# Keys and values of block 2 as seven half-size products, and one megabyte of an expert's weights in the router's places

## The reference, cut to what matters

```python
u = rmsnorm(h, norm1_g)
proj = u @ w_in                      # 1024 -> 6656 columns
cb, cc, cx, q, k, v, gc, ga = split_columns(proj)   # q 1024 wide, k and v 256 each
...
h = h + merged @ w_o
hf = rmsnorm(h, norm2_g)
# 64 experts of width 512, two per token, chosen from hf @ w_group and hf @ w_router
y = (silu(xb @ w1[e]) * (xb @ w3[e])) @ w2[e]
```

## Time and profile before

| | |
|---|---|
| median of 3 runs | 1544.93 us (1544.66 to 1547.16) |
| the profiled execution | 1545.07 us, of which the span is 1543.2 us |
| PE busy | 1247.8 us (81%) |
| DVE, ACT, POOL busy | 549.4, 246.7, 18.2 us |
| loaded from memory | 499.78 MB, 325 GB/s over the span |
| mean granted TensorE clock | 0.917 of full speed |

### The profile page before, as it was taken

One profiled execution on the slowest core, in us unless ns is written; L12 is line 12 of the kernel. 1 busy time (PEld: TensorE's weight loads), 2 busy tenths in 40 slices (PEclk: granted clock), 3 DMA queues, 4 the chain that ended last, 5 costly groups with the idle time before them and its releaser, 6 DMA issues.

```text
span 1543.2 us, 18891 instructions
## 1 busy us (share of the span) xinstructions
PE 1247.8 (81%) x8005; PEld 706.6 (46%) x8005; DVE 549.4 (36%) x1115; ACT 246.7 (16%) x710; POOL 18.2 (1%) x30
## 2 busy tenths in 40 slices
PE   8999999999999999996765775775676576577477
PEld 5665899944699544542232232232232233223223
DVE  6644578795756667421111111111111111111111
ACT  2434213211234101211010010010000001001001
POOL 2000000000000000100000000000000000000000
PEclk9999999999999999998888898788798789788889
DMA  9631746406433686999999999999999999999997
GB/s 305 217 111 55 244 153 217 162 30 217 163 112 113 236 303 237 374 429 428 429 429 429 428 429 428 428 429 428 429 429 428 428 429 428 429 429 429 429 426 327
DMA packets 93859, 501.53 MB, mean 325 GB/s; under 512 B 6845, under 2 KB 34865, under 8 KB 68464
## 3 DMA queue, kind: packets, MB, share of 16 engines
q1 hardware_dynamic: 93040, 500.00, 79.9%
q0 software_dynamic: 768, 0.85, 0.2%
HBM read 499.78 MB, written 1.05 MB: 325 GB/s over the span
## 4 chain that ended last, share of the span: by engine, by line
PE 58%; DMA 39%; DVE 2%; issue 1%; ACT 1%; SPq 0%; DVEq 0%
DMA arena<-in_w 38%; PE ps L1754 18%; PE ps L1329 8%; PE ps L1558 6%; PE ps L1553 4%; PE ps L1366 3%; PE ps L928 2%; PE ps L1139 2%; PE ps L933 2%; PE ps L978 2%; PE ps L1494 2%; PE ps L1654 1%; PE ps L1279 1%; PE ps L1432 1%; PE ps L955 0%
## 5 line engine op out<-in xcount | busy, mean ns | idle before, releaser
L1754 PE MATMUL ps<-arena,hT 128*32 128x512 f32 x1984 | 277.8, 723 | 252.7 <-DMA arena<-in_w 252.7
L1754 PEld LDWEIGHTS ps<-arena,hT 128*32 128x32 f32 x1984 | 69.2, 130 | 460.8 <-issue 319.3
L3006 DVE TENSOR_TENSOR moe_hid<-moe_hid,ps 64x512 f32<-64x512 f32 x32 | 22.1, 690 | 480.8 <-ACT moe_hid L3407 480.8
L1776 PE MATMUL ps<-arena,moe_turned 128*32 128x512 f32 x1024 | 118.3, 601 | 28.0 <-DVE moe_turned L3008 27.9
L1734 PEld LDWEIGHTS ps<-sel,h 128*128 128x128 f32 x992 | 113.2, 192 | 24.1 <-issue 24.1
L3407 ACT ACTIVATE moe_hid<-ps 64x512 f32<-64x512 f32 x32 | 18.8, 588 | 655.9 <-PE ps L1754 650.3
L1734 PE MATMUL ps<-sel,h 128*128 128x64 f32 x992 | 117.2, 276 | 0.0
L3391 ACT ACTIVATE hT<-ps,gcol 128x64 f32<-128x64 f32 x252 | 55.0, 328 | 156.8 <-PE ps L1734 156.8
L3008 DVE COPY moe_turned<-ps 128x512 f32<-128x512 f32 x32 | 22.1, 692 | 161.8 <-PE ps L1765 161.8
L1776 PEld LDWEIGHTS ps<-arena,moe_turned 128*32 128x32 f32 x1024 | 32.9, 110 | 88.7 <-issue 72.0
L1329 PE MATMUL ps<-arena 128*128 128x128 f32 x640 | 73.1, 275 | 0.0
(11 more groups left out here) (499 smaller groups left out, 1427.3 us busy)
## 6 DMA issues: line engine op xcount, KB each, us to landing
arena<-in_w SPq DMA_DIRECT2D x182, 2048.0 KB, 29.4
arena<-in_w_in SPq DMA_DIRECT2D x18, 2048.0 KB, 9.1
arena<-in_w_up SPq DMA_DIRECT2D x22, 1024.0 KB, 9.0
arena<-in_w SPq DMA_DIRECT2D x17, 1024.0 KB, 12.9
arena<-in_w_down SPq DMA_DIRECT2D x5, 2048.0 KB, 13.5
arena<-in_w_out SPq DMA_DIRECT2D x2, 2048.0 KB, 15.2
arena<-in_w_conv_out SPq DMA_DIRECT2D x2, 2048.0 KB, 7.7
arena<-in_w_attn_out SPq DMA_DIRECT2D x2, 2048.0 KB, 11.9
```

The source lines that it names most:

```text
L1754: last = mm(ps[k * CAP:(k + 1) * CAP, UP, :], x[:, c, (k % 2) * CAP:(k % 2 + 1) * CAP], w[:, at:at + DE], start=(c == 0), stop=(c == KC - 1))
L1776: last = mm(ps[k * CAP:(k + 1) * CAP, DN, :], a[:, m * 64 + (k % 2) * CAP:m * 64 + (k % 2 + 1) * CAP], w[:, at:at + 512], start=(m == 0), ...
```

## The change

1. **Keys and values.** `kv2` becomes seven products of half the rows, half the inner dimension and half the columns (256), in banks 0 to 3, interleaved with those of the queries: kv 1, the first half of q 1, the turn of the tokens, the rest of q 1, kv 2, kv 5, 6, 7, q 2, kv 3, kv 4, q 5, 6, 7, 3, 4. DVE makes the four weight sums of `kv2` around its share of the first token half (`norm_take(2, 0)`), and five sums of results; ACT copies two. `q_first_w_sums` moves behind the left-side sums.
2. **Release.** `release_last` is gone from this place. `dense_used` is raised for `kv2` in product 5 of the queries, after a wait for all seven kv products.
3. **The megabyte.** `xg` shrinks to the first quarter of `hT`. The first half of w3 of expert 3 goes, behind `load_behind_wo` and after the router's products, into the other three quarters of `hT` (0.75 MB) and into `router_w` (0.25 MB). Its second half goes into slot 0 at the first `quarter_used`; the load at the second is gone. In pair 1 `expert_up` takes the fourth matmul's weights from these places.
4. **Pairs 1 and 2** are written out for PE, and the loop has 14 turns for pairs 3 to 30.

The products, sums and outputs are the same otherwise. The core of the diff (the constants for semaphore counts, the tile views and the removed `part` branches are left out):

```diff
+ORDER_Q, ORDER_KV = [1, 2, 5, 6, 7, 3, 4], [1, 2, 5, 6, 7, 3, 4]
...
-        LOOPED = range(1, PAIRS - 1)
+        LOOPED = range(3, PAIRS - 1)
...
-        xg = hT[:, :, 0:2 * CAP]
+        hT_flat = hT.rearrange("p c s -> p (c s)")
+        xg = hT_flat[:, 0:KC * 2 * CAP].rearrange("p (c s) -> p c s", c=KC)
+        ahead = [hT_flat[:, at:at + DE] for at in (512, 1024, 1536)] + [router_w.rearrange("p c n -> p (c n)")[:, 0:DE]]
...
+            def load_ahead():
+                sp.wait_ge(logits_ready, 2)
+                sp.dma_start(hT_flat[:, 512:2048], t["w3"][3, :, 0:3 * DE]).then_inc(piece_in, 16)
+                sp.dma_start(ahead[3], t["w3"][3, :, 3 * DE:4 * DE]).then_inc(piece_in, 16)
...
                         load_behind_wo()
+                        load_ahead()
                         sp.wait_ge(quarter_used, 1)
-                        sp.dma_start(MOE_SLOTS[0][:, 0:2048], t["w3"][3, :, 0:2048]).then_inc(moe_loaded[0], 16)
-                        moe_wait(1, 3)
-                        sp.dma_start(MOE_SLOTS[0][:, 2048:4096], t["w3"][3, :, 2048:4096]).then_inc(moe_loaded[0], 16)
+                        sp.dma_start(MOE_SLOTS[0][:, 0:2048], t["w3"][3, :, 2048:4096]).then_inc(moe_loaded[0], 16)
...
+            def kv(product):
...
+                if product in (5, 6, 7, 4):
+                    pe.wait_ge(kv_summed, count1(KV_SUMS, {5: "t1", 6: "t2", 7: "t3", 4: "t4"}[product]))
...
+                if product == 2:
+                    pe.wait_ge(seven_copied, KV_COPIED)
+                if product in (3, 4):
+                    pe.wait_ge(kv_summed, count1(KV_SUMS, {3: "c22", 4: "u2"}[product]))
+                for c in range(4):
...
+                    last = mm(kv_bank(product), lhs, rhs, start=(c == 0 and product not in (2, 3)), stop=(c == 3),
+                              skip_group_check=True)
+                last.then_inc(kv_filled, 1)
+
+            def queries(product, chunks=range(4)):
...
+                if product in (3, 4):
+                    pe.wait_ge(seven_sums, count7(-1, SUMS7, {3: "c22", 4: "u2"}[product]))
+                for c in chunks:
...
+                    if product == 5 and c == 0:
+                        pe.wait_ge(kv_filled, len(ORDER_KV))
+                        pe.sem_inc(dense_used, 1)
+                if 3 in chunks:
                     last.then_inc(seven_filled, 1)
+
+            def kv_and_queries():
+                wait_hT(16)
+                kv(1)
+                queries(1, (0, 1))
+                norm_turn(2, xn2, 1)
+                queries(1, (2, 3))
+                kv(2)
+                wait_hT(20)
+                for product in (5, 6, 7):
+                    kv(product)
+                queries(2)
+                kv(3)
+                kv(4)
+                for product in (5, 6, 7, 3, 4):
+                    queries(product)
...
+                        if second and k == 3:
+                            w, at = (units[3], (c - 4) * DE) if half else (ahead[c], 0)
...
+            kv_w_sum("t1")
             norm_take(2, 0)
+            for name in ("t3", "t2", "t4"):
+                kv_w_sum(name)
             dve.wait_ge(ff_down, 5)
...
                 v.tensor_tensor(q_x[:, 1], q_x[:, 0], a11, ALU.subtract).then_inc(x_sums7_ready, 1)
+                dve.wait_ge(x_sums7_ready, count7(-1, X_SUMS7, "s2"))
+                v.tensor_tensor(q_x[:, 3], a12, q_x[:, 1], ALU.subtract).then_inc(x_sums7_ready, 1)
+                q_first_w_sums()
+                for name in ("u2", "u3", "c22"):
+                    kv_sum(name)
                 dve.wait_ge(w_sums7_ready, count7(-1, W_SUMS_UP, "t3"))
                 v.tensor_tensor(b12, b22, q_t1, ALU.subtract).then_inc(w_sums7_ready, 1)
...
                 v.tensor_tensor(w_sum_b, b21, b12, ALU.subtract).then_inc(w_sums7_ready, 1)
+                kv_sum("c12")
+                kv_sum("c21")
                 turn_tables()
                 keys()
                 first_w_sums(0, (1,))
...
                 elif kind == "seven":
+                    act.wait_ge(kv_filled, count1(ORDER_KV, 1))
+                    a_(kv_u2, kv_bank(1), ACT.Copy).then_inc(seven_copied, 1)
```

More of the change, by code:

```diff
@@ L168 @@
 ORDER7 = [5, 1, 6, 7, 2, 3, 4]
-SCHEDULE2 += [("part", "kv2", _q) for _q in range(4)] + [("seven", 0, 0)]
+SCHEDULE2 += [("seven", 0, 0)]
 SCHEDULE2 += [("product", "cc", _p) for _p in ORDER7]
@@ L202 @@
 ORDER_UP = [1, 5, 6, 7, 2, 3, 4]
+ORDER_Q, ORDER_KV = [1, 2, 5, 6, 7, 3, 4], [1, 2, 5, 6, 7, 3, 4]
+KV_COPIED = 2 * UP_SETS + 2
+KV_SUMS = ["t1", "t3", "t2", "t4", "u2", "u3", "c22", "c12", "c21"]
 W_SUMS_UP = ["t1", "t3", "t2", "t4"]
@@ L478, in up_seven_bank, with kv_bank, kv_columns @@
             return ps[:, up_bank(m) + BANK7[product], :]
+        def kv_bank(product):
+            return ps[:, BANK7[product], 0:256]
+        def kv_columns():
+            w = dense_slot("kv2").rearrange("p (c n) -> p c n", c=KC)
+            return w[:, 0:4, 0:256], w[:, 0:4, 256:512], w[:, 4:8, 0:256], w[:, 4:8, 256:512]
         def bank7(g, product):
@@ L1473, in attend @@
                         pe.sem_inc(attn2_done, 1)
-            def q_seven():
-                for n in ("q0", "q1"):
-                    pe.wait_ge(dense_loaded[RING_SLOT[UNIT[n]]], dense_loads(UNIT[n]))
-                b11, b12, b21, b22 = q_columns()
[L1481 to L1497, removed]
-                    last.then_inc(seven_filled, 1)
@@ L1578, in _ @@
             for kind, a, q in SCHEDULE2:
[L1579 to L1585, removed]
+                if kind == "product":
                     seven_product(SET[a], q, hT, release_q if a == "cc" else lambda: release_seven(SET[a] - 1))
@@ L1747, in gather_first, with expert_up @@
                     last.then_inc(gathered, 1)
-            def expert_up(x, units, halved, half, done):
+            def expert_up(x, units, halved, half, done, second=False):
                 for c in range(4 * half, 4 * half + 4):
@@ L1838, in pair_step @@
                         wait_unit(p, k)
+                    if p == 1 and not half:
+                        pe.wait_ge(piece_in, 64)
                     if p and not half:
@@ L1897, in pair_turn @@
                 expert_down(aT, units, False, 1, y_filled)
-            pair_step(0)
+            for p in range(LOOPED[0]):
+                pair_step(p)
             with nc.tensor.Fori(0, len(LOOPED) // 2) as i:
-                pair_turn(1, i)
-                pair_turn(2, i)
+                pair_turn(LOOPED[0], i)
+                pair_turn(LOOPED[1], i)
             pair_step(PAIRS - 1)
@@ L2475, in _, with kv_w_sum @@
             norm_rows(2, xn2, 0)
+            def kv_w_sum(name):
+                b11, b12, b21, b22 = kv_columns()
+                if name == "t1":
+                    u = UNIT["kv2"]
+                    dve.wait_ge(dense_loaded[RING_SLOT[u]], dense_loads(u))
+                if name == "t2":
+                    dve.wait_ge(kv_summed, count1(KV_SUMS, "t1"))
+                if name == "t4":
+                    dve.wait_ge(kv_summed, count1(KV_SUMS, "t2"))
+                x, y = {"t1": (b12, b11), "t3": (b22, b12), "t2": (b22, kv_t["t1"]), "t4": (b21, kv_t["t2"])}[name]
+                v.tensor_tensor(kv_t[name], x, y, ALU.subtract).then_inc(kv_summed, 1)
+            kv_w_sum("t1")
             norm_take(2, 0)
+            for name in ("t3", "t2", "t4"):
+                kv_w_sum(name)
             dve.wait_ge(ff_down, 5)
@@ L2523, in queries, with kv_sum @@
                 v.memset(tail[:, 3:4], 0.0).then_inc(roped2, 1)
[L2525 to L2530, removed]
+            def kv_sum(name):
+                dst, r, product = {"u2": (kv_u2, kv_u2, 6), "u3": (kv_u3, kv_u2, 7), "c22": (v2[:, 1, :], kv_u3, 5),
+                                   "c12": (v2[:, 0, :], kv_u2, 3), "c21": (z2[:, 1, 1024:1280], kv_u3, 4)}[name]
+                dve.wait_ge(kv_filled, count1(ORDER_KV, product))
+                if name == "u2":
+                    dve.wait_ge(seven_copied, KV_COPIED)
+                else:
+                    dve.wait_ge(kv_summed, count1(KV_SUMS, {"u3": "u2", "c22": "u3", "c12": "u2", "c21": "u3"}[name]))
+                done = bank_emptied_dve if name == "c21" else kv_summed
+                v.tensor_tensor(dst, r, kv_bank(product), ALU.add).then_inc(done, 1)
             def cw2(tap, c):
@@ L2799, in q_sum @@
                 v.tensor_tensor(dst, r, ps[:, 4 + BANK7[product], :], ALU.add).then_inc(seven_sums, 1)
-            dve.wait_ge(hT_act, 20)
-            q_first_w_sums()
             for kind, a, q in SCHEDULE2:
-                if kind == "part":
-                    if q % 2 and PRODUCTS[PROD[a]][1][q // 2] == "D":
-                        empty2(a, q // 2)
-                elif kind == "product":
+                if kind == "product":
                     if a == "cc":
@@ L3247, in _ @@
             norm_take(2, 1)
-            def empty2(name, bank):
-                b = filled_bank(name, bank)
```

(8 more changed lines are left out.)

66 lines of the change are left out of this document (48 added, 18 removed).

## The result

The changed kernel takes 1553.22 us (median of six runs, 1551.45 to 1554.68) against 1545.71 us for the kernel before on the same chip (1544.66 to 1547.71): 1.0046 times as long, 95% interval 1.0036 to 1.0056. The forecast was 1551.0 us and "slower"; the first median lies 0.2 us above its range, the second inside it.

A forecast was written before the change was run, and what follows sets the result against it. PE bounds the kernel to about 670 us, then loads set the end, so PE's dense-part time counts. 1545.07 - 1.65 + 5.99 + 2.2 - 0.6 = 1551.0 us; 0.80 chance within 1547.5 to 1553.0.

The forecast's parts named there:

- 6 to 7 were named as a sign: Sign in the changed profile: the first `cc` product comes 6 to 7 us later than 411.07.
- Fewer columns: kv2 on PE: 56 instructions of 256 columns take 12.08 us in place of 13.73, saving 1.65 us.
- The sums of kv: kv's weight sums and copies on DVE and ACT lie beside PE and cost nothing; up to 0.7 us without cover.
- The later release: `cc1` issued at 392.37 reaches DVE at 401.66; the queries' c22 comes late, and PE waits 5.99 us before product 3.
- The clock: PE's granted clock falls in the wait, slowing the queries' products 3 and 4: 2.2 us, range 1.5 to 3.0.
- The rival in which it holds: The clock holds through PE's gap: 1547.7 to 1549.4 us, chance 0.18.
- the one in which it stays low through both products: Clock stays at 1.2 GHz through the queries' products 3 and 4: 6.87 us more, 1556.3 us, chance 0.03.
- The megabyte: Loads ahead fill part of a 0.72 MB hole from 641 to 649 us: 0.6 us gained, range 0 to 1.7.
- That `cc1` would not hold DVE: Rival: `cc1` is in place when DVE asks at 397.7, PE waits only 2.0 us: 1544.8 us, chance 0.11.
- The point from which PE's lost microseconds pass to the end: A microsecond on PE before 640 us moves the end by a microsecond; in the expert part it moves nothing.

The follow-up runs named there:

- third: Changed kernel with the queries' u2, u3, c22 put ahead of the sums that wait for `cc1` in DVE's order: 1546.42 us, ratio 1.0001.
- fourth experiment: Changed kernel with kv 3 and 4 ahead of the queries' product 2, the release moved up, ACT's copy of product 2 later: 1547.68 us, ratio 1.0012.
- second profile: Profile of the changed kernel run again unchanged, in a later set of runs: 1552.70 us, ratio 1.0043.
- the eighth experiment: Kernel before with eight unused products of 512 columns on PE ahead of the queries' product 3: 1552.33 us, ratio 1.0040.
- The second: Kernel before with only the megabyte loaded ahead and pairs 1 and 2 written out: 1545.92 us, ratio 1.0001.
- the ninth experiment: Changed kernel run again unchanged, beside the filled wait without the megabyte: 1552.70 us, ratio 1.0043.

## Why the prediction was right

Its sum was -1.65 + 5.99 + 2.2 - 0.6 = +5.9 us. The stage of the first profile by the same terms, without the megabyte, is -1.59 + 4.92 + 1.72 = +5.05. So the first product of `cc` comes 5 us later within the stage, where 6 to 7 were named as a sign. The mechanism is the one that was forecast; the wait and the clock came out smaller, and the megabyte gave nothing.

- **Fewer columns: right.** The 56 instructions took 1.73 + 1.78 + 5.18 + 3.45 = 12.14 us (kv 1; kv 2; kv 5, 6, 7; kv 3, 4), against 12.08 forecast. The Trainium skill (TensorE: Matmul & The Clock Gate, Back-to-back issue gap), from whose figures 18.0 us were worked out, does not hold for this stream.
- **The sums of kv: right.** PE had no gap between kv 1 and the queries' product 7, which ended about 30.2 us after the stage's start (30.13 forecast).
- **The later release: right in every link, 1.07 us too long.** The term took 9.29 us from the issue of `cc1` to DVE, as the kernel before has it; the changed kernel has 8.1. The rest of the chain fits: `cc1` was issued 20.0 us after the start (19.95 forecast), and from DVE's t1 to the end of c22 it took 6.88 us, as forecast. The third and fourth experiment took away one link each, and the gap fell to 1.67 and 1.66 us.
- **The clock: right.** It fell in the gap, and products 3 and 4 were 1.72 us longer (2.2 forecast, 1.5 to 3.0 in its range); 1.49 of this was the clock, 1.93 in the second profile. With the wait filled it did not fall. The rival in which it holds is out, and so is the one in which it stays low through both products: it was back after 3 to 4 us.
- **The megabyte: wrong.** "0.72 MB or 1.7 us are to be had" read a rate of 338 GB/s as a hole, beside a DMA share of 0.94 in the same row. With the megabyte ahead the rate rose by 8 to 18 GB/s and not by 90, most of what is missing lies in the run-up that the prediction named for its lower end, and neither pair of runs within one set shows a gain in time (1545.92 beside 1545.80, 1544.43 beside 1543.88 us). The term is zero within what the medians can tell, as the lower end had it.
- **Not in the sum:** the ending at low clock, about 1.6 us, was in both profiles of the changed kernel; whether the change brings it stays open. With it, 5.05 to 5.56 us for the two stages make 6.6 to 7.2, and the ratios 1.0046 and 1.0043 are 7.1 and 6.6 us. The terms that were too large and this missing one nearly cancel; that the forecast is 1.7 to 2.2 us from the medians, and not more, owes something to that, which is luck.
- **The rivals.** That `cc1` would not hold DVE needed a landing within 5.3 us of the issue; it took 8. The point from which PE's lost microseconds pass to the end was right: the eighth experiment lost 6.87 us on PE and 6.5 in the median.

## What to carry to other kernels

When work is split so that a buffer is given back later, follow the next load into that buffer to the engine that asks for it first, and then down that engine's list: what stands behind the waiting instruction, though it needs nothing of the load, is late too. The cure is an order, not a faster piece: results that another engine waits for go ahead of sums that wait for a load, and a product that needs neither goes into the wait. Before bytes are moved into a "hole" in the loads, read the busy share of the DMA engines beside the rate; here a rate of 338 GB/s at a share of 0.94 was no hole of 0.72 MB.

## What the runs showed of the hardware that was not expected

TensorE's clock was low without any idle time of PE in the profile before it: from 92 to 99 us PE was busy for all 7 us, as it had been for the 8 us before, at 0.51 of the clock in the changed kernel's profile and 0.52 in the eighth experiment's, but at 1.00 in that of the kernel before. The second and the ninth experiment's profiles have a shorter such stretch there (0.78 and 0.82). In the changed kernel's first profile it cost 1.45 us on one group of 16 instructions alone (5.10 for 3.65). The 8 us before it:

```profile
84.00:92.00 8.00, 8.00 (x64) 6.40 (x63) 1.44 (x6) 0.60 (x1) 0.00 (x0) 1.00 0.00 0
```

Gaps of 1.66 and 1.67 us on PE left the granted clock at 1.00, and those of 4.92, 4.94 and 5.00 did not; in these three profiles it fell about 4.5, 4.7 and 2.0 us after PE stopped and cost 1.49, 1.58 and 1.93 us, so nearly equal gaps did not cost the same. Ten instructions without use in such a gap kept the clock at 1.00, and the products behind them took 7.10 us for 8.59.
